# A float32 model kernel: the weight remainders of the 26 early input tiles formed by GpSimd in its loop instead of by VectorE

## The reference, cut to what matters

```python
h = jnp.concatenate([meta, x], axis=1)              # 272 x 1024
u = rmsnorm(h, norm1_w[l])
proj = u @ w_in[l]                                  # 1024 x 6672: 52 tiles of 128 channels and dt
hg_q, hg_f, hg_i, hg_g, m2_z, m2_xbc, m2_dt = jnp.split(proj, PROJ_SPLITS, axis=-1)
out_a = hgrn2_mixer(...)                            # gated linear attention, 8 heads
out_b = mamba2_mixer(...)                           # conv of 4 taps over m2_xbc, then a scan by dt
h = h + jnp.concatenate([out_a, out_b], axis=-1) @ w_out[l]
h = h + conv_glu_ffn(rmsnorm(h, norm2_w[l]), ...)   # 1024 -> 2 x 2816 -> 1024
```

## Time and profile before

| | us |
|---|---|
| median of 3 runs | 1693.16 (1692.19 to 1694.89) |
| the profiled execution | 1690.15 |
| its span | 1688.4 |

### The profile page before, as it was taken

How to read it: one execution, slowest core, us unless ns; L and a number is a source line. 1 busy time by engine, 2 the same in 40 slices (tenths; PEclk the granted TensorE clock), 3 DMA queues, 4 the chain that set the end, 5 groups by cost and what they waited for, 6 DMA issues and landing times.

```text
span 1688.4 us, 20775 instructions
## 1 busy us (share of the span) xinstructions
PE 1309.5 (78%) x8366; PEld 773.0 (46%) x8366; DVE 513.8 (30%) x938; ACT 477.9 (28%) x714; POOL 232.1 (14%) x100
## 2 busy tenths in 40 slices
PE   8989999999999999988666665666666666666565
PEld 5877788889999988843111111111111111111111
DVE  4864667436667545622000000000000000000001
ACT  5753566346564534722000000000000000010001
POOL 0000000038768654300000000000000000000000
PEclk9999999999999999988888888878878888877887
DMA  8846322268445542286999999999999999999996
GB/s 278 330 151 249 123 101 80 87 211 272 151 141 217 205 150 100 101 363 268 428 429 428 429 429 428 428 429 429 429 429 428 429 429 428 429 429 429 429 428 269
DMA packets 92480, 524.01 MB, mean 310 GB/s; under 512 B 8026, under 2 KB 31090, under 8 KB 64514
## 3 DMA queue, kind: packets, MB, share of 16 engines
q1 hardware_dynamic: 92369, 523.13, 76.4%
q10 hardware_dynamic: 48, 0.01, 0.0%
HBM read 522.08 MB, written 1.05 MB: 310 GB/s over the span
## 4 chain that ended last, share of the span: by engine, by line
DMA 47%; PE 42%; DVE 7%; ACT 3%; issue 1%; POOL 0%; SPq 0%; DVEq 0%; ACTq 0%
DMA ring<-in_w_down 24%; DMA ring<-in_w_up 23%; PE ps L671 6%; PE ps L675 6%; PE ps L672 6%; PE ps L895 5%; PE ps L1244 3%; PE ps L919 3%; PE ps L1263 3%; PE ps L1152 2%; PE ps L655 1%; PE ps L729 1%; DVE arena L2085 1%; PE ps L825 1%; ACT ring_r L1303 1%
## 5 line engine op out<-in xcount | busy, mean ns | idle before, releaser
L1244 PE MATMUL ps<-ring,arena 128*32 128x512 f32 x1984 | 292.8, 728 | 175.2 <-DMA ring<-in_w_up 126.0
L1650 POOL TENSOR_TENSOR ring_r<-ring,ring_r 128x1024 fp32r<-128x1024 f32 (+1 forms) x96 | 231.9, 2436 | 473.0 <-ACT ring_r L1303 473.0
L671 PE MATMUL ps<-arena_r,ring_r 128*128 128x258 f32 (+3 forms) x960 | 288.5, 301 | 8.7 <-PE ps L675 3.3
L675 PE MATMUL ps<-arena_r,ring_r 128*128 128x258 f32 (+3 forms) x960 | 280.7, 292 | 0.0
L1263 PE MATMUL ps<-ring,arena 128*32 128x512 f32 x1024 | 172.4, 809 | 102.5 <-DMA ring<-in_w_down 94.8
L1244 PEld LDWEIGHTS ps<-ring,arena 128*32 128x32 f32 x1984 | 62.0, 122 | 374.4 <-DMA ring<-in_w_up 189.1
L671 PEld LDWEIGHTS ps<-arena_r,ring_r 128*128 128x128 f32 x960 | 182.4, 190 | 19.6 <-issue 12.5
L675 PEld LDWEIGHTS ps<-arena_r,ring_r 128*128 128x128 f32 x960 | 181.7, 189 | 2.8
L672 PE MATMUL ps<-arena_r,ring_r 128*128 128x256 f32 (+2 forms) x608 | 180.1, 296 | 0.0
L1303 ACT ACTIVATE ring_r<-ring 128x1024 fp32r<-128x1024 f32 (+1 forms) x122 | 126.0, 1037 | 40.3 <-PE ps L672 21.4
L1263 PEld LDWEIGHTS ps<-ring,arena 128*32 128x32 f32 x1024 | 32.9, 129 | 224.6 <-DMA ring<-in_w_down 147.3
(11 more groups left out here) (383 smaller groups left out, 1393.2 us busy)
## 6 DMA issues: line engine op xcount, KB each, us to landing
ring<-in_w_gate SPq DMA_DIRECT2D x64, 2048.0 KB, 25.9
ring<-in_w_down SPq DMA_DIRECT2D x64, 2048.0 KB, 26.3
ring<-in_w_up SPq DMA_DIRECT2D x60, 2048.0 KB, 24.7
ring<-in_w_in SPq DMA_DIRECT2D x20, 2048.0 KB, 11.6
ring<-in_w_ada SPq DMA_DIRECT2D x12, 2048.0 KB, 8.6
ring<-in_ffn_w_up SPq DMA_DIRECT2D x22, 1024.0 KB, 7.8
ring<-in_w_out SPq DMA_DIRECT2D x6, 2048.0 KB, 8.1
ring<-in_ffn_w_down SPq DMA_DIRECT2D x4, 2048.0 KB, 8.3
```

The lines of the kernel that those rows point to most:

```text
L671: pe.matmul(o, hi[:, k, :], r_(xhi(k0 + k)), start=first and k == 0, stop=False)
L675: mm = pe.matmul(o, lo[:, k, :], r_(xhi(k0 + k)), start=False, stop=last and k == nk - 1)
L1244: mm = pe.matmul(ps[32 * j:32 * j + 32, half, :], xs[:, kt, :], wk[:, 512 * j:512 * j + 512], start=kt == 0, stop=kt == KT - 1)
L1650: pool.tensor_tensor(r_(w), w, f_(rounded(c)), ALU.subtract).then_inc(ev("w_lo"), 1)
```

## The change

GpSimd's loop no longer skips the first 26 chunks, `in_rest` and its three calls are gone from VectorE, and TensorE waits for `w_lo` for every chunk. `in_lo` now counts only the eight remainders of the input. Nothing is added to ScalarE or to the transfers, and what is computed is the same.

```diff
@@ split_products, TensorE
                 c = CH[name]
-                if c < len(SPLIT):
-                    pe.wait_ge(ev("in_lo"), 1 + c + KT * (c > 0))
-                else:
-                    pe.wait_ge(ev("w_lo"), c - len(SPLIT) + 1)
+                pe.wait_ge(ev("w_lo"), c + 1)
@@ the projection loop, TensorE
-                                        x_ready=1 if j == SPLIT[0] else None, ready="in_lo")
+                                        x_ready=0 if j == SPLIT[0] else None, ready="in_lo")
@@ GpSimd
             for c, (_, w) in enumerate(chunks):
-                if c < len(SPLIT):
-                    continue
                 pool.wait_ge(ev("w_hi"), c + 1)
                 pool.tensor_tensor(r_(w), w, f_(rounded(c)), ALU.subtract).then_inc(ev("w_lo"), 1)
@@ VectorE, before the loop
-            def in_rest(j):
-                c = CH[f"i{j}"]
-                w = chunks[c][1]
-                dve.wait_ge(ev("w_hi"), c + 1)
-                tt(r_(w), w, f_(rounded(c)), ALU.subtract).then_inc(ev("in_lo"), 1)
-            in_rest(SPLIT[0])
             for k in range(KT):
                 dve.wait_ge(ev("u_hi"), k + 1)
                 tt(r_(uin(1, k)), uT[:, k, :], f_(uin(0, k)), ALU.subtract).then_inc(ev("in_lo"), 1)
-            in_rest(SPLIT[0] + 1)
@@ VectorE, in the loop over j
-                if j + 3 in SPLIT and j + 3 > SPLIT[1]:
-                    in_rest(j + 3)
```

## The result

The changed kernel is slower: a median of 1698.99 us (1696.87 to 1701.32) against 1692.31 us (1689.57 to 1694.89) of the kernel before, six runs of each, a ratio of 1.0039 with a 95% interval of 1.0027 to 1.0051. In a later session beside other kernels it came to 1700.91 us, 1.0048 (1.0035 to 1.0061).

A forecast was written before the change was run, and what follows sets the result against it. DMA (47%) and TensorE (42%) bound the kernel, so TensorE's early losses reach the end: 5.6 + 3.2 - 0.9 + 0.3 - 1.0 + 1.5 = +8.7 us on the 1693.16 median gives 1701.9, range 1692 to 1711.

The forecast's parts named there:

- part 3: Projections 4 to 15: convolution steps wait for GpSimd's subtractions, so VectorE takes up the dt rows later, +5.6 us.
- part 4: The dt chain on VectorE: two GpSimd subtractions, i16 and i17, stop its small SBUF steps, +3.2 us.
- part 5: The scan behind the dt chain: VectorE freed of remainders but partly meeting GpSimd, -0.9, +0.3 and -1.0 us.
- part 6: TensorE's granted clock: one more fall to 0.50 behind new idle stretches, +1.5 us (bounds -1.4 and +4.5).
- Part 1: At i4 TensorE starts about 1.0 us later, later covered (inside part 3); i2 and i3 stay covered.
- Part 2: VectorE steps with two SBUF inputs or fast SBUF-to-SBUF copies exclude GpSimd's subtraction, which holds for 2.06 us.
- the walk of convolution 4: Part 3's step-by-step timing of the convolutions: convolution 4 ends at 53.9 us, then 10.7 us for three tiles.
- No absorption behind: After the first 120 us: shifts at 160 us and at the end differ by no more than 2 us.
- (a): Rival: convolution steps are not held up and only the gain counts, -3.3 to -4.7 us, about 1689; chance 0.10.
- (b): Rival: exclusion mostly absorbed, dt chain meets one subtraction, parts 3 and 4 total 3 to 5 us, 1693 to 1697; chance 0.15.
- (c): Rival: 3.8 us a tile, several clock falls, scores meet GpSimd too, +15 to +20 us, 1708 to 1713; chance 0.15.

The follow-up runs named there:

- after_again: The changed kernel without any edit, run again in a later session beside other kernels: 1700.91 us, ratio 1.0048 to the kernel before.
- after: The changed kernel in its first session, against the kernel before: 1698.99 us, ratio 1.0039.
- first_two_vector: The changed kernel with the remainders of i2 and i3 alone back on VectorE: 1699.2 us, ratio 1.0041 to the kernel before.
- conv_psum: The changed kernel with the 36 convolution steps reading their second input from PSUM, so not the convolution: 1693.49 us, ratio 0.9993 to the kernel before.
- conv_on_vector: The changed kernel with the remainders of i4 to i15 back on VectorE: 1692.11 us, ratio 0.9999 to the kernel before.
- par_copies_early: The changed kernel with VectorE's three parameter copies moved from behind convolution 3 to behind convolution 0: 1697.45 us, ratio 1.0029 to the kernel before.
- conv_psum_before: Control: the kernel before with the convolution steps reading their second input from PSUM: 1692.03 us, ratio 0.9994 to the kernel before.
- late_order: The kernel before with VectorE's remainders from round 15 on put behind each step of the scan: 1687.19 us, ratio 0.9974 to the kernel before.
- gpsimd_from_18: The changed kernel with the remainders of i2 to i17 back on VectorE: 1689.84 us, ratio 0.9978 to the kernel before.
- dt_on_vector: The changed kernel with the remainders of i16 and i17 alone back on VectorE: 1697.39 us, ratio 1.0022 to the kernel before.

## Why the prediction was right, and where not

The forecast, 1701.9 us, had the sign, the mechanism and most of the size; the first median is 2.9 us below it, the second 1.0 us. By its own steps, measured between the profiles of before and of after_again:

| step | predicted | measured |
|---|---|---|
| part 3, to the start of the dt rows | +5.6 | +7.35 |
| part 4, the dt chain | +3.2 | +2.92 |
| part 5, from the dt result to the states | -0.9 | -0.36 |
| part 5, states to heads | +0.3 | +0.34 |
| part 5, heads to second spreading | -1.0 | -0.97 |
| part 6, a further fall of the clock | +1.5 | 0.2 to 0.5, inside the -0.36 |
| sum | +8.7 | +9.28 |

**Part 1** held: i4 came late (ScalarE's rounding at 37.56 in after, its DMA 1.15 us later than in the earlier trace rows, but at 36.53 in after_again), and i2 and i3 are covered, as first_two_vector shows. Of the +10.0 us in the first profile about 1 us is that DMA.

**Part 2**, the rule for the sum, was the step that decided, and it was read from a stage that the change doesn't touch. conv_psum, its control and conv_on_vector show it from both sides: take the second SBUF input away, or the subtraction, and the loss at the dt rows is gone but for 0.7 to 1.0 us. The Trainium skill (SBUF — State Buffer, SBUF: two separate sides) says that of the two engines whichever starts first gets the pair of ports they share for the whole instruction; the trace agrees with the blocking, and puts the end of the hold 0.2 us before the end of GpSimd's row each time.

**Part 3** was mis-sized by 1.7 us. The pace was right: convolution 7 to 10 took 10.7 us in after_again (67.54 to 78.27) as predicted. The step that failed is the walk of convolution 4, in which I had left out the three parameter copies of that round, 0.58 us; they let the next subtraction in first and cost 2.8 us there. About 1.1 us came back before the dt rows. par_copies_early shows it. The 7.35 us itself leans on an early profile: from the rounding of i4 to the dt rows it is 44.16 us in after and in after_again, and 36.93 in the kernel before, but 37.02, 37.82 and 38.31 in conv_psum_before, late_order and gpsimd_from_18, which form the same remainders on VectorE up to there. So the price of the part is 5.9 to 7.2 us, and the walk's +5.6 is nearer to it than the table says. The prediction had this part down as its least sure one, but for another reason, the length of the hold, which was right.

**Part 4** held within 0.3 us, shown by dt_on_vector.

**Part 5** held to 0.5 us, and most of that is the clock. In six other profiles, in which it was at 0.50 for less of this stretch or not at all, the way from the dt result to the states takes 11.76 to 11.79 us, 0.9 less than in the kernel before, as forecast. One detail was wrong: the subtractions hold the first of the two staging steps only, never both.

**Part 6** was wrong as a price of this fall. It came where it was expected, but TensorE was not what the stretch behind it waited for. So the two errors, 1.7 us too little in part 3 and about 1 us too much in part 6, cancelled in large part by luck; the sum is better than its terms. The 1.5 us for a fall is of the right size where TensorE is the bound (1.3 us in conv_psum_before).

**No absorption behind.** The claim that the shift at 160 us is that of the end within 2 us held in after: +10.0 at the second spreading, +10.05 at 800 us, +9.93 at 1556 us, +11.1 at the end. In after_again it is less clean: +9.3 at the second spreading, +12.5 at ScalarE's step at 177 us because of the late fall of the clock, and +10.6 at the end, so about 2 us of a loss were absorbed behind it there.

**From the profile to the median.** The profiled spans differ by 11.1 us, the medians by 6.7 and 8.6. The profiled execution of the kernel before was 2 us under its own median and early in just this stretch (control: 118.98 instead of 117.20); that of after was 2.3 us over its own. A sum worked out from positions of one such trace carries that; adding the 3.0 us between the profiled execution and the median is why 1701.9 stands above both medians.

**The rivals.** (a), GpSimd is free, falls with the first row of L1733. (b), mostly absorbed: the dt chain met two subtractions, not one, and parts 3 and 4 came to 10.2 us. (c), it bites harder: of the twelve score steps L1824 only one was held in after (2226 ns), the one that part 5 counts, and three convolutions took the 10.7 us of the walk, not the 11.4 us of 3.8 us a tile. Its falls of the clock did come in part, but by execution: the fall at 170 us in after_again cost 3.3 us, and after had none there.

## What to carry to other kernels

Before work is moved to GpSimd, look for a place in the same trace where GpSimd already runs beside VectorE and compare, line by line, the steps with two SBUF inputs with those that read one from PSUM: the difference between mean and median there is the price, and it is paid by such steps in the new place, not by the work that moves. A linked chain loses one whole hold for each subtraction that begins inside it (12 of the 36 convolution steps stood, beside the 12 subtractions of i4 to i15), and a few tenths of a microsecond decide which side gets in first. Where what one wants is only that a long step no longer stands ahead of a critical one in a queue, moving it behind that step on its own engine gave 5.1 us here. Moving everything to the idle engine lost 6.7, and moving there only what stood ahead of the scan's steps (i18 to i27) gave 3.4.

## What the runs showed of the hardware

Even steps on 16 partitions are blocked in full: 16x272 took 2.51 instead of 0.29 us. The cast of 48x272 from SBUF to SBUF took 1.86 us beside a subtraction. Steps with one PSUM input took at most 499 ns in conv_psum, beside the same subtractions. GpSimd in turn pays little: its subtraction takes 2.39 us with a blocked step beside it and 2.53 to 2.60 where a step has slipped in ahead. And the price of a granted clock of 0.50 depends on who is waited for: 0.2 to 0.5 us at 95 to 101 us in after and after_again, where the next step waited for VectorE, 1.3 us at 92 to 97 us in conv_psum_before, and 3.3 us at 170 to 177 us in after_again.
